# Two attention input projections rewritten in the seven-product form

## What is computed

```python
# x: (1, 512, 1024), w_in: (1024, 3072)
h = rms_norm(x, norm1_g[i]) * (1.0 + sc1) + sh1
q, k, v = jnp.split(h @ w_in, 3, axis=-1)      # both attentions
# layer 0: differential attention (8 heads, two maps of 64), layer 1: stick-breaking attention (16 heads of 64)
x = x + g1 * (attention(q, k, v) @ w_out)
```

## Times and profile before

| | us |
|---|---|
| median of 3 runs | 2445.83 (2444.72 to 2456.11) |
| the profiled execution | 2447.63 |
| its span, first to last instruction | 2445.9 |
| TensorE busy | 2209.7 |
| VectorE busy | 759.0 |
| ScalarE busy | 435.7 |

### The profile page before, as it was taken

The page is one execution under the profiler, slowest core; times in us unless marked ns, Lnnn a source line. Parts: engine busy times, 40 slices in busy tenths (PEclk is TensorE's granted clock), DMA queues, the critical chain, the costliest instruction groups (busy, mean ns, idle before and its releaser), DMA issues. The chain is left out here.

```text
span 2445.9 us, 24138 instructions
## 1 busy us (share of the span) xinstructions
PE 2209.7 (90%) x9430; PEld 1149.7 (47%) x9430; DVE 759.0 (31%) x1552; ACT 435.7 (18%) x817; POOL 262.3 (11%) x508
## 2 busy tenths in 40 slices
PE   8999999999999998998877777899899988888777
PEld 4354448888864445563322222344454733222222
DVE  2255625666432019241111111310472411000113
ACT  2222411000011017111000000110472211000001
POOL 3122102000000002111111100000131111111110
PEclk9999999999999999999999999999999999999999
DMA  7568826121231112179999999920003699999995
GB/s 267 181 206 275 289 84 243 69 104 69 81 138 69 69 38 101 44 304 420 407 427 428 421 417 421 346 72 0 35 1 138 236 417 416 427 428 427 427 422 238
DMA packets 128608, 586.91 MB, mean 240 GB/s; under 512 B 17960, under 2 KB 29616, under 8 KB 103436
## 3 DMA queue, kind: packets, MB, share of 16 engines
q1 hardware_dynamic: 113056, 548.72, 56.2%
q0 software_dynamic: 14864, 36.76, 4.1%
q10 hardware_dynamic: 604, 0.27, 0.1%
HBM read 571.31 MB, written 30.65 MB: 246 GB/s over the span
## 5 line engine op out<-in xcount | busy, mean ns | idle before, releaser
L2186 PE MATMUL ps<-ring,arena 128*64 128x512 f32 x1920 | 452.3, 612 | 95.7 <-ACT arena L2235 52.0
L2186 PEld LDWEIGHTS ps<-ring,arena 128*64 128x64 f32 x1920 | 142.8, 140 | 374.6 <-issue 281.2
L250 PE MATMUL ps<-hT,ring 128*128 128x512 f32 (+3 forms) x688 | 286.6, 578 | 4.2 <-issue 4.2
L2224 PE MATMUL ps<-ring,arena 128*64 128x512 f32 x960 | 239.9, 658 | 48.4 <-DMA ring<-in_expert_w_down 36.0
L250 PEld LDWEIGHTS ps<-hT,ring 128*128 128x128 f32 (+1 forms) x688 | 128.0, 190 | 161.0 <-issue 157.2
L257 PE MATMUL ps<-ring,hT 128*128 128x512 f32 x448 | 196.3, 597 | 0.1
L2264 DVE TENSOR_TENSOR arena<-ps,arena 128x512 f32<-128x512 f32 x32 | 22.1, 692 | 517.2 <-PE ps L2186 517.2
L2224 PEld LDWEIGHTS ps<-ring,arena 128*64 128x64 f32 x960 | 79.3, 151 | 188.3 <-issue 172.4
L1182 PE MATMUL ps<-hT,ring 128*128 128x256 f32 x640 | 141.6, 379 | 0.0
L257 PEld LDWEIGHTS ps<-ring,hT 128*128 128x128 f32 x448 | 85.2, 192 | 105.1 <-issue 104.5
L2269 DVE TENSOR_TENSOR arena<-ps,arena 128x1024 f32<-128x1024 f32 x30 | 36.7, 1225 | 310.4 <-PE ps L2224 310.4
(11 more groups left out here) (406 smaller groups left out, 2688.5 us busy)
## 6 DMA issues: line engine op xcount, KB each, us to landing
ring<-in_expert_w_gate SPq DMA_DIRECT2D x60, 2048.0 KB, 17.6
ring<-in_expert_w_up SPq DMA_DIRECT2D x58, 2048.0 KB, 17.1
ring<-in_expert_w_down SPq DMA_DIRECT2D x58, 2048.0 KB, 19.1
ring<-in_ada_w SPq DMA_DIRECT2D x24, 2048.0 KB, 11.1
ring<-in_diff_w_in SPq DMA_DIRECT2D x6, 2048.0 KB, 13.6
ring<-in_sb_w_in SPq DMA_DIRECT2D x6, 2048.0 KB, 20.0
ring<-in_ffn_w_gate SPq DMA_DIRECT2D x5, 2048.0 KB, 12.1
ring<-in_ffn_w_val SPq DMA_DIRECT2D x5, 2048.0 KB, 8.2
```

What stands on the lines that cost most here:

```text
L250: mm = pe.matmul(out, w[:, c, cols], x[:, c, :], start=(c == 0), stop=(c == chunks - 1))
L2186: mm = pe.matmul(k.ps[slots, 2 + kind, :], k.xT[:, c, slots], w[:, c, :], start=(c == 0), stop=(c == KD - 1))
L2224: mm = pe.matmul(k.ps[slots, 5 + half, :], k.hTt[:, c, slots], w[:, c, half * 512:(half + 1) * 512], start=(c == 0), stop=(c == KH - 1))
```

## The change

Both projections keep `tokens` jobs for the first half of the values (piece 4). The second half (piece 5) becomes seven products of 8 calls with 256 columns. The features become groups of two tiles, seven products of 4 calls with 256 columns: 8 groups in the first attention, 7 in the second, which keeps query features 6 and 7 as jobs. VectorE makes four input sums (1024 elements a partition), four value sums (1024) and four sums a group (512); the sums and two first products lie in ring slots 4 and 5, and w22 - w12 is written over w12 in the piece. The pieces now rotate through four slots, `w_out` apart. The wait of SP for `halves` in the second part goes.

```diff
-QKV_PIECES = {"diff": ((4, 8), (5, 8), (0, 12), (1, 16), (2, 20), (3, 24)),
-              "sb": ((4, 8), (5, 8), (1, 24), (0, 15), (2, 19), (3, 23))}
+VALUE_BANK = {1: 0, 2: 1, 5: 2, 6: 3, 4: 4, 7: 5, 3: 6}
+VALUE_PRODUCTS = (1, 2, 5, 6, 4, 7, 3)
+VALUE_EVACS = 3
+QKV_PLAIN = (TT, TT + 1)
+QKV_GROUPS = (tuple((2 * g, 2 * g + 1) for g in range(8)),
+              ((4, 5), (0, 1), (2, 3), (8, 9), (10, 11), (12, 13), (14, 15)))
+QKV_PIECES = {"diff": ((4, 4), (5, 5), (0, 7), (1, 9), (2, 11), (3, 13)),
+              "sb": ((4, 4), (5, 6), (1, 14), (0, 9), (2, 11), (3, 13))}
...
 def qkv_tensor(pe, k, a, turns, besides={}):
-    for j in range(QKV_JOBS - a.late_jobs):
...
-        if j < 8:
...
-            tokens(pe, qkv_bank(k, j), k.hT, j // 2, a.stream.view(a.first_piece + j % 2)).then_inc(a.proj, 1)
-        else:
-            feature_job(pe, k, a, j)
...
+    for tt in range(TT):
+        if tt in turns:
+            turn_tensor(pe, k, a.norm, turns[tt])
+        if tt in besides:
+            besides[tt]()
+        hT_ready(pe, a.norm, tt + 1)
+        tokens(pe, k.ps[:, tt, :], k.hT, tt, a.stream.view(a.first_piece)).then_inc(a.proj, 1)
+    if a.flip:
+        a.stream.wait(pe, feature_piece(a, 6))
+        single_feature(pe, k, a, 6, 7).then_inc(a.proj, 1)
...
+    inputs = {1: k.hT[:, low, FIRST_HALF], 2: k.hT[:, high, FIRST_HALF], 3: s4, 4: k.hT[:, high, LAST_HALF], 5: s1, 6: s2, 7: s3}
...
+    weights = {1: w11, 2: w21, 3: w22, 4: t4, 5: t1, 6: t2, 7: w12}
+    mixed = {5: 1, 6: 2, 7: 3, 3: 4}
+    summed = {5: 1, 6: 2, 4: 3, 7: 4}
...
+    for n in VALUE_PRODUCTS:
...
+        for tt in range(2):
+            for c in range(4):
+                mm = pe.matmul(value_bank(k, a, n)[:, tt * 256:(tt + 1) * 256], inputs[n][:, c, tt * P:(tt + 1) * P],
+                               weights[n][:, c, :], start=(tt == 0 and c == 0), stop=(c == 3), skip_group_check=True)
...
+    for g in range(len(a.groups)):
...
+        for n in PRODUCTS:
+            if n == PRODUCTS[0]:
+                pe.wait_ge(a.evac, a.evac_at + (1 if g == 0 else VALUE_EVACS + max(g - 1, 0)))
+            if n == 7 and g == 0:
+                pe.wait_ge(a.evac, a.evac_at + 2)
+            if n == 4:
+                pe.wait_ge(a.first_out, a.first_at + g + 2)
+            if n == 5:
+                pe.wait_ge(a.sums, a.sums_at + 4 + g + 1)
...
+            for c in range(4):
+                mm = pe.matmul(out, weights[n][:, c, :], inputs[n][:, c, :], start=(n in BANK_FIRST and c == 0), stop=(c == 3),
+                               skip_group_check=True)
...
+def group_sums_vector(dve, k, a, ch, g):
...
+    ch.link(dve.tensor_tensor(t1, w12, w11, ALU.subtract))
+    ch.link(dve.tensor_tensor(t2, w22, t1, ALU.subtract))
+    ch.mark(dve.tensor_tensor(w12, w22, w12, ALU.subtract))
+    dve.tensor_tensor(t4, t2, w21, ALU.subtract).then_inc(a.sums, 1)
...
+def qkv_vector(dve, k, a, ch):
+    hT_ready(dve, a.norm)
+    a.stream.wait(dve, a.first_piece + 1)
+    for n in range(4):
+        input_sum(dve, k, a, n)
+        value_sum(dve, k, a, n)
...
+    group_sums_vector(dve, k, a, ch, 1)
+    for g in range(len(a.groups)):
+        group_evacuated_vector(dve, k, a, ch, g)
+        if g + 2 < len(a.groups):
+            group_sums_vector(dve, k, a, ch, g + 2)
...
-    pe.wait_ge(a.proj_act, QKV_JOBS // 2)
-    pe.wait_ge(a.proj_dve, QKV_JOBS // 2)
+    groups = len(a.groups)
+    pe.wait_ge(a.proj_act, TT + groups // 2)
+    pe.wait_ge(a.evac, a.evac_at + VALUE_EVACS + groups - 1)
     scores(0)
     for i in range(DIFF_STEPS):
+        if i == 2:
+            pe.wait_ge(a.evac, a.evac_at + VALUE_EVACS + groups)
...
-def plan_attention(st, a, w_in, w_out):
+def plan_attention(st, a, w_in, w_out, out_slots):
     for n, used in QKV_PIECES[a]:
         st.add([piece(st, rows_strided(w_in), n * 512, 512)], a, "proj", used)
+    st.rotate(*out_slots)
...
             for n in range(8):
-                if n == 4:
-                    sp.wait_ge(first.halves, 2)
                 a.stream.load(sp, n)
...
-            qkv_tensor(pe, k, a, {0: 0, 1: 1, 3: 2, 5: 3}, {j: lambda tt=j + 2: placed_tensor(pe, k, t, first, tt) for j in range(2)})
+            qkv_tensor(pe, k, a, {tt: tt for tt in range(TT)}, {j: lambda tt=j + 2: placed_tensor(pe, k, t, first, tt) for j in range(2)})
...
+        for slot in SCRATCH_SLOTS:
+            k.stream1.lend(slot, "diff", "evac", FFN_EVACS + VALUE_EVACS + len(QKV_GROUPS[0]))
+        plan_attention(k.stream1, "diff", w["diff_w_in"][0], w["diff_w_out"][0], SCRATCH_SLOTS)
         k.stream2 = Stream(k, k.stream1.landed, k.stream1.count)
-        plan_attention(k.stream2, "sb", w["sb_w_in"][0], w["sb_w_out"][0])
+        k.stream2.rotate(0, 1, 2, 3)
+        plan_attention(k.stream2, "sb", w["sb_w_in"][0], w["sb_w_out"][0], (0, 1))
```

More of the change, by code:

```diff
@@ L1443, in qkv_out @@
[L1443 to L1451, removed]
-def qkv_scalar(act, k, a):
[L1455 to L1462, removed]
@@ new lines, with value_bank, group_bank, feature_piece @@
+QKV_PIECES = {"diff": ((4, 4), (5, 5), (0, 7), (1, 9), (2, 11), (3, 13)),
+              "sb": ((4, 4), (5, 6), (1, 14), (0, 9), (2, 11), (3, 13))}
+def value_bank(k, a, n):
+    return k.ps[:, (VALUE_BANK[n] + 4 * a.flip) % 8, :]
+def group_bank(a, g):
+    return 4 * ((g + a.flip) % 2)
+def feature_piece(a, f):
+    return a.first_piece + a.piece_at[f // 4]
+def qkv_blocks(w, second, first):
+    low, high = slice(0, 4), slice(4, 8)
+    return w[:, low, first], w[:, low, second], w[:, high, first], w[:, high, second]
@@ new lines, in group_blocks, with value_blocks, value_mix, group_mix @@
+def group_blocks(k, a, g):
+    second, first = (slice(f % 4 * P, (f % 4 + 1) * P) for f in a.groups[g])
+    return qkv_blocks(a.stream.view(feature_piece(a, a.groups[g][0])), second, first)
+def value_blocks(k, a):
+    return qkv_blocks(a.stream.view(a.first_piece + 1), slice(256, 512), slice(0, 256))
+def value_mix(k):
+    return [k.qkv_mix[:, n * 1024:(n + 1) * 1024].rearrange("p (c n) -> p c n", n=256) for n in range(3)]
+def group_mix(k, g):
+    flat = k.qkv_mix[:, g % 2 * 1536:g % 2 * 1536 + 1536]
+    return [flat[:, n * 512:(n + 1) * 512].rearrange("p (c n) -> p c n", n=P) for n in range(3)]
@@ new lines, in qkv_scalar @@
+def qkv_scalar(act, k, a):
+    for tt in range(TT):
+        act.wait_ge(a.proj, tt + 1)
+        act.copy(k.v[:, tt, 0:512], k.ps[:, tt, :]).then_inc(a.proj_act, 1)
+    if a.flip:
+        act.wait_ge(a.proj, TT + 1)
+        act.mul(k.q[:, 6, :], k.ps[:, 7, :], a.q_scale[6]).then_inc(a.proj_act, 1)
+    act.wait_ge(a.prod, a.prod_at + 1)
+    act.copy(k.value_first, value_bank(k, a, 1)).then_inc(a.first_out, 1)
+    for g in range(len(a.groups)):
+        act.wait_ge(a.prod, a.prod_at + 6 + 3 * g + 1)
+        if g:
+            act.wait_ge(a.evac, a.evac_at + VALUE_EVACS + g)
+        act.copy(k.group_first, k.ps[:, group_bank(a, g) + 3, 0:HALF_T]).then_inc(a.first_out, 1)
+        if g and a.groups[g - 1][0] < 8:
+            for f in a.groups[g - 1]:
+                ins = act.mul(k.q[:, f, :], k.q[:, f, :], a.q_scale[f])
+            ins.then_inc(a.proj_act, 1)
@@ new lines, in value_sum @@
+def value_sum(dve, k, a, n):
+    w11, w12, w21, w22 = value_blocks(k, a)
+    t1, t2, t4 = value_mix(k)
+    if n:
+        dve.wait_ge(a.sums, a.sums_at + min(n, 2))
+    if n == 0:
+        ins = dve.tensor_tensor(t1, w12, w11, ALU.subtract)
+    elif n == 1:
+        ins = dve.tensor_tensor(t2, w22, t1, ALU.subtract)
+    elif n == 2:
+        ins = dve.tensor_tensor(t4, t2, w21, ALU.subtract)
+    else:
+        ins = dve.tensor_tensor(w12, w22, w12, ALU.subtract)
+    ins.then_inc(a.sums, 1)
@@ new lines, in input_sum @@
+def input_sum(dve, k, a, n):
+    low, high = slice(0, 4), slice(4, 8)
+    a11, a21, a12, a22 = k.hT[:, low, FIRST_HALF], k.hT[:, low, LAST_HALF], k.hT[:, high, FIRST_HALF], k.hT[:, high, LAST_HALF]
+    s1, s2, s3, s4 = k.qkv_inputs
+    if n == 0:
+        ins = dve.tensor_tensor(s1, a21, a22, ALU.add)
+    elif n == 1:
+        dve.wait_ge(a.mixed, a.mixed_at + 1)
+        ins = dve.tensor_tensor(s2, s1, a11, ALU.subtract)
+    elif n == 2:
+        ins = dve.tensor_tensor(s3, a11, a21, ALU.subtract)
+    else:
+        dve.wait_ge(a.mixed, a.mixed_at + 2)
+        ins = dve.tensor_tensor(s4, a12, s2, ALU.subtract)
+    ins.then_inc(a.mixed, 1)
@@ new lines, in group_sums_vector @@
+def group_sums_vector(dve, k, a, ch, g):
+    w11, w12, w21, w22 = group_blocks(k, a, g)
+    t1, t2, t4 = group_mix(k, g)
+    a.stream.wait(dve, feature_piece(a, a.groups[g][0]))
+    if g < 2:
+        dve.wait_ge(a.prod, a.prod_at + 5)
+    else:
+        dve.wait_ge(a.proj, QKV_PLAIN[a.flip] + g)
+    ch.link(dve.tensor_tensor(t1, w12, w11, ALU.subtract))
+    ch.link(dve.tensor_tensor(t2, w22, t1, ALU.subtract))
+    ch.mark(dve.tensor_tensor(w12, w22, w12, ALU.subtract))
+    dve.tensor_tensor(t4, t2, w21, ALU.subtract).then_inc(a.sums, 1)
```

(27 more changed lines are left out.)

115 lines of the change are left out of this document (81 added, 34 removed).

## The result

The changed kernel takes 2418.84 us (median of 4 runs, 2415.13 to 2425.2) and the kernel before, beside it, 2445.27 us: a ratio of 0.9888, interval 0.9868 to 0.9909. The forecast was 2417.3 us, range 2411 to 2428. The profiled execution took 2415.13 us (span 2413.4) where that of before took 2447.63 (span 2445.9).

The account below looks back on a forecast made before the run. The prediction took both projections to be bound by TensorE. Its terms, -16.0 - 14.4 + 3.4 - 0.8 - 0.7 = -28.5 us, gave 2419.1 us as a profiled execution, 2417.3 us from the median; range 2411 to 2428.

Parts of the forecast that it names:

- part 1: Matmuls of both projections: fewer 512-column records, more 256-column ones in seven products; -16.0 us first attention, -14.4 us second.
- rival d: Projection matmuls: weight loads aren't hidden, 0.190 us on top of every record; slower, 2501 us; chance 0.01.
- part 2: VectorE and ScalarE in both projections: added sums and evacuations stay hidden; 0, bounds 0 and 3 us for each attention.
- Rival (b): Group starts in both projections: VectorE's evacuations 1 us late, 15 groups give 15 us back, 2432 us; chance 0.07.
- part 3: Weight pieces of both projections: in the new ring order they land before they are needed; 0, bounds -1 and +3 us.
- part 4: Second attention's token tiles 2 and 3: a gap from turn to tokens, +1.7 us twice; +3.4 us, bounds 0 and 6.
- rival (a): Token tiles of the second attention: the clock falls at the new gaps, 2 us each, 2421 us; chance 0.10.
- part 5: Ends of both projections: scores follow the last group at once; -0.8 us first, -0.7 us second, bounds -1.5 and +1 each.
- rival c: Expert loop: changed rounding adds an expert pair, 31.5 us; 2449 us, with one in each layer 2480; chance 0.02.

Follow-up runs that it names:

- The eighth product: Changed kernel with the last product of each group and of the value half issued twice; one run, 2452.34 us, beside 2452.91 us for the kernel before.
- the runs with more sums: Changed kernel with four or twelve repeats of a 512-element VectorE sum ahead of each group's own; one run each, 2417.89 us and 2444.38 us.
- the kernel that applies the second part only: Kernel with the change in the second attention alone, the first attention's projection as in the kernel before; 2438.73 us, ratio 0.9948 to the kernel before.
- the two edges: Changed kernel with second-attention turns of tiles 2 and 3 two calls earlier and the late evacuation moved behind the first softplus; 2412.72 us, ratio 0.9856.

## Why the prediction was right

*Matmuls (part 1, -16.0 and -14.4).* Right. First projection: four token jobs of 6.9 us, then 560 records without idle. Starts forecast for the first products, the groups and the scores were 772.4, some 797 and 893; they came at 770.55, 794.72 and 891.51, 1.5 to 2.3 us earlier, about the 1.9 us that everything upstream was. The eighth product shows that the eighth is the whole of it, to about 1 us.

*Weight loads not hidden (rival d).* False (its sum took 0.213 us for the pitch in place of its own 0.2155, 1.4 us too little for the first projection, which changes nothing): 504 loads of 95.57 us lie beside 108.87 us of matmuls, and the eighth product's records cost 0.216 us with their loads. The rule of the Trainium skill ("TensorE: Matmul & The Clock Gate", The mechanism), that a load overlaps only where the row groups differ, would have these full-row loads add up; the trace disagrees here as it did in the earlier trace rows. The same section also has loads pulled ahead where they go to the background weight buffer; that sentence agrees with the trace, though no run here shows the buffer itself.

*VectorE (part 2, 0).* Right. Eight sums ahead of the products at 1.14 us apart, 9.1 us in all where 9.8 to 11.0 were taken, done at 1584.4 against product 5 at 1596.0. (The prediction gives times of the second attention on the scale of the kernel before, where its projection starts 22.1 us later.) VectorE's timeline at the end of the second attention's value products and in its first groups:

```profile
1616.20 0.68 DVE L1610 TENSOR_TENSOR ring<-ring 128x512 f32<-128x512 f32 x1
1620.45 0.69 DVE L1664 TENSOR_TENSOR arena<-ring,ps 128x512 f32<-128x512 f32 x1 [3.56 <-PE ps L1535]
1623.90 0.69 DVE L1667 TENSOR_TENSOR arena<-arena,ps 128x512 f32<-128x512 f32 x1 [2.77 <-PE ps L1535]
```

It waits 3.56 and 2.77 us for TensorE inside one group. Rival (b), late evacuations at the groups' starts, is false; the runs with more sums show that it begins somewhere between four and twelve more.

*Pieces (part 3, 0).* Right: L144's pieces of the first attention went from 681.2 to 794.9 us, those of the second from 1527.9 to 1613.5, none took over 20.6 us to land, and no new product waited for one. One time was off without a price: the second attention's last output piece went at 1698.1 us, right behind the last product, which is 1720 on the prediction's scale, where 1710 stood. No matmul of the output projection waited for it.

*Token tiles (part 4, +3.4).* The mechanism is right, two gaps of 1.60 us for ScalarE's half of hT, and so is the size, 3.2 us. The clock didn't fall at them (16 records in 7.13 us behind each, and 1.00 granted in the window that holds both), so rival (a) is false as put.

*Ends (part 5, -0.8 and -0.7).* The first is there: TensorE starts the scores at 891.51, as the last product ends; with the old projection, in the kernel that applies the second part only, it stood 0.88 us before them. VectorE's first score operation starts 0.7 us behind the last matmul, as forecast. For the second the 0.73 us are gone too. What the forecast didn't see is the late product's evacuation, which holds VectorE behind a wait of 5.97 us; the old kernel's order had the same wait, so it cost the change nothing, but 3.1 us lay there.

*One more expert pair (rival c).* False: 1920 and 960 records in the two expert lines, as before.

*The sum.* Projections -29.1 us against -28.5. By the medians -26.4 us beside the kernel before, by the profiled executions -32.5. The forecast sits between. The two profiled executions have the same form of the router, and the 3.4 us that they have beyond the projections are the stages' own spread. Which form the runs without a trace had isn't known. That the medians show less because more of the changed kernel's four runs had the longer form fits their times (two of four at 2422 us and above, against one of four, at 2456, before), but it isn't shown. So the mechanism and its size were forecast, and that the median came within 1.5 us of 2417.3 is in part luck: the router's 7 us weren't in the sum, and they fit in the range only because it had been left some 17 us wide for other causes.

## What to carry to other kernels

Where a stage is bound by TensorE without idle and a matmul's pitch is proportional to its columns, as in the rows here (0.4272 us at 512, 0.2155 at 256), the seven-product form gives back one eighth of the matmuls it is applied to and no more; count the records that stay outside it. In these projections the sums were free: VectorE needs 5.3 us in the 12.1 us of seven products, and they were still free when it needed some 8.2. A wait put ahead of ready work in an engine's list can cost time even where the wait itself is harmless, 3.1 us here: look at each long wait of an engine for what is queued behind it. And before a difference of a few us between medians is explained, compare two traces of one kernel by stages.

## What the runs showed of the hardware

VectorE's operation of 192 elements took 0.36 us in five traces and 3.25 in four. GpSimd's addition of 1024 elements (2.36 us) started some 0.67 us after the operation's start in all nine; in the five the operation was over by then, in the four it ended 0.2 us behind the addition. That the two engines got in each other's way fits the rows, but it wasn't tried apart from this. In these four TensorE's granted clock had already fallen in the router before it (7.68 to 8.57 us in place of 6.05 for 52 filler records, at 0.69 to 0.78 of the clock in place of 1.00), and not behind a longer idle time: in the two traces of the changed kernel TensorE stood for 0.20 us (clock fell) and 0.22 us (it didn't) ahead of this stretch. Why the clock falls there in one execution and not in the other, and whether VectorE's long operation comes of it, stays open.

The clock after an idle time isn't set by the length of the idle time alone. Ahead of the second attention's token tiles TensorE stood for 2.33 to 2.43 us in every trace, then turned a tile and ran four records. In the changed kernel:

```profile
1543.68 1.13 PE L206 MATMUL ps<-ident,arena 128*128 128x128 f32 x8 [2.42 <-DVE arena L198]
1544.64 1.88 PE L2527 MATMUL ps<-arena 128*128 128x512 f32 x4
```

and before, behind 2.33 us of idle, the four took 3.56 us. With four more sums, a kernel with the same TensorE stream as the changed one, they took 3.28 us behind 2.43. The granted clock over the four records is 1.00 in the changed kernel, 0.52 before and 0.55 with four more sums. So 1.88 us (2.4 GHz) and up to 3.56 us (most of it at 1.2 GHz) both follow the same wait. It is worth at most 1.7 us, and it accounts for the 1.16 us that the head of the second attention seemed to gain: the head is 18.5 us in the five traces with 1.88 us (the changed kernel twice, twelve sums, the eighth product, the two edges) and 19.6 to 19.8 in the other four.
